# Second norm of a one-layer decoder step: x added on GpSimd ahead of the second projection part, squares taken at once, tile groups of 2, 2, 4, 4, 4, and 14 slots for the conditioning loads

## The chip, the cores and the metric

The kernel runs on one core of a Trainium2 chip. The metric is the device time of one execution in microseconds (us). TensorE (PE) multiplies matrices, VectorE (DVE) and ScalarE (ACT) work element by element, GpSimd (POOL) does some of that too, and SyncE (SP) issues most of the transfers (DMAs) from memory.

## The reference

One layer of a hybrid decoder over 256 prompt tokens and 8 samples of 4 tokens (288 columns in all), in float32. The conditioning vector gives six rows of shifts, scales and gates per sequence:

```
mod = silu(c) @ ada_w + ada_b
sh1, sc1, g1, sh2, sc2, g2 = split(mod, 6)
h = rms_norm(x) * (1 + sc1) + sh1
mix = token_mixer(h)            # ends with: out = merged @ w_out
x = x + g1 * mix
h = rms_norm(x) * (1 + sc2) + sh2
ff = conv_ffn(h)                # up = h @ w_up; conv, gelu, gate; @ w_down
x = x + g2 * ff
y = rms_norm(x, final_norm_w)
```

D_MODEL is 2048 (16 tiles of 128 rows), D_FF is 5632. The change concerns the stretch from the end of `merged @ w_out` to the first columns of `h @ w_up`: the residual sum, the second norm and its modulation, and the last eight blocks of `mod`.

## The kernel before

Activations lie transposed, 128 rows of a tile on the partitions and 288 token columns beside each other. A weight matrix is read in chunks of 512 rows by 256 columns (512 KB) into a ring `raw` of four. ScalarE rounds a chunk to its high part `whi` (line 1258, function `hi`), VectorE takes the low part `wlo` (line 1691, `lo`), and TensorE makes three products for each of eight (row tile, column half) pairs: high by high, high by low, low by high (lines 767 to 769). A chunk is 24 matmuls of 288 columns. The same split is made of the activations, `xh` and `xl`. The bank pair `ps` holds two output blocks in turn, and `bank_free` tells TensorE that a block has been read.

Each engine runs its own list of instructions in order, and semaphores join them. The order is written by hand.

The output projection has two passes. P1 (24 chunks) covers 12 of the 16 row tiles of `merged`; its results, times the gate g1, go to `mixo`. P2 (8 chunks, one for each output block u) covers the last four row tiles. `second_part(u)` on VectorE adds P2's result times the gate to `mixo` (line 2078, two operations out of PSUM), reads the sample columns into `x1s` (line 2079, which frees the bank) and adds them (line 2081). GpSimd then adds x, brought back from a spill into `xT2` (line 2399). ScalarE squares four tiles at a time (line 1611), and GpSimd sums the first twelve tiles' squares to four in `sqacc` (line 2404). TensorE sums the squares over the rows by multiplying with `ones` (line 1173): four times `sqacc` and four times the last tiles' squares. Square root on ScalarE (line 1286), reciprocal on VectorE (line 1841), then by groups of four tiles: normalise (line 1739, VectorE), sample columns modulated (lines 1750 and 1752, VectorE), prompt columns modulated (line 1304, ScalarE), high part (line 1310, ScalarE), low part (line 1758, VectorE). The first up chunk needs the first group, the second chunk the second, and so on.

Meanwhile the last eight blocks of conditioning are computed. A fill n is four chunks of `ada_w` (512 KB each) multiplied by the conditioning columns `cs` into a PSUM region (line 793); ScalarE copies the rows out (`fill_rows`, line 1261), TensorE turns them (`fill_turn`, line 746), VectorE reduces and stores them (`ada_block`, lines 1706 and 1713). Fills 0 and 1 lie inside P2, ahead of chunks 4 and 6; fills 2 and 3 behind P2, 4 and 5 behind the sum of squares, 6 and 7 ahead of up chunks 1 and 3. The turns of blocks 2 to 7 lie ahead of up chunks 3 to 8. The chunks of the fills land in ten slots taken in turn. SP issues them (line 693) between the up stream's loads (line 616), each behind the wait that its slot or ring place needs; a wait on SP holds up all that follows on it.

Between fill 5 and the first up chunk TensorE makes 16 transposes of the identity (`WARM`, line 1180). The up stream has 16 chunks for the first pair of blocks and ten more rounds of 16 in a loop; on ScalarE its step n makes the high part of chunk n + 3 first, then what else is due. GpSimd spills the new x from `xT2` to memory (line 2411) when the second group's low part is done; the down stream reads it again, and `ffl` later takes the place of `xT2`.

Of the kernel before, what the change touches and what calls it, by code (L numbers as in the profile page):

```python
# [21 lines left out]
P = 128  # L22
# [28 lines left out]
ZAB_Y = 4  # L51
# [69 lines left out]
FRING = 10  # L121
FILL_P2 = {4: 0, 6: 1}
FILL_UP = {1: 6, 3: 7}
# [53 lines left out]
WARM = 16  # L177
# [82 lines left out]
def build(nc, x_prompt, x_sample, c_prompt, c_sample, state_hgrn, state_mlstm_C, state_mlstm_n, state_mlstm_m,  # L260
# [5 lines left out]
    with ExitStack() as ctx:  # L266
# [143 lines left out]
        afill = sb("afill", [P, FRING - 4, KC, CN], stack=post)  # L410
# [148 lines left out]
        def fill_slot(e):  # L559


            r = e % FRING
            return araw[:, r] if r < 2 else top[:, r - 2] if r < 4 else afill[:, r - 4]

        def fill_landed(e):


            r = e // 2 % 5
            return (ld_x, 48) if r == 4 else (u_landed[r], 32 * UNITS + 16 * EXTRA * (r < 2))

        def fill_acc(n):


            o = CN * (n in (3, 4))
            return ab[:, 0:CN] if n in (0, 6) else R[:, (None, 2, 1, 1, 2, 2, None, 0)[n], o:o + CN]
# [38 lines left out]
        def _(sp):  # L614
# [74 lines left out]
            def fill_loads(a, b):  # L689
                for e in range(a, b):  # L690
                    if e >= FRING:
                        sp.wait_ge(a_used, before_a(A_UP) + e - FRING + 1 + FREE)
                    sp.dma_start(fill_slot(e), ada_v[:, KC * (e % 4):KC * (e % 4 + 1), bass.ds(CN * (A_UP + e // 4), CN)]).then_inc(fill_landed(e)[0], 16)
# [18 lines left out]
            first_up(0, 1, 2)  # L712
            fill_loads(10, 14)
            first_up(3)
            fill_loads(14, 24)
            first_up(4)
            fill_loads(24, 28)
            first_up(5)
            fill_loads(28, 32)
            first_up(*range(6, 16))  # L720
# [21 lines left out]
        def _(pe):  # L742
# [72 lines left out]
            def fill(n):  # L815
# [9 lines left out]
                if n == 6:  # L825
                    pe.wait_ge(ada_free, UNITS + A_UP - A_HG + 2 + FREE)
                if n == 7:
                    pe.wait_ge(rs_done, 3)
                for c in range(4):
                    e = 4 * n + c  # L830
                    if c % 2 == 0:
                        pe.wait_ge(fill_landed(e)[0], fill_landed(e)[1] + 32 * (e // FRING + 1))
# [6 lines left out]
            def stream(N, kinds, a0=None, steps=None, length=4, kt0=0, xparts=None, halves=None, start=False, ahead_of=None):  # L839

                steps = nothing() if steps is None else steps
                for k, kind in enumerate(kinds):
                    if kind == "s":
# [10 lines left out]
                        else:  # L854
                            if s == 0:
                                pe.wait_ge(bank_free[b % 2], N[1] + b // 2 + (PARTED // 2 - PARTED // 8) * start + FREE)
                            if xparts is not None and b == 0:
# [302 lines left out]
            def p2_ahead(q):  # L1160
                if q == 6:
                    fill_turn(0)
                if q in FILL_P2:
                    fill(FILL_P2[q])
            stream(N_P2, "s" * 8, length=1, kt0=12, halves=XS + 4, ahead_of=p2_ahead)
            fill(2)
            fill(3)
            fill_turn(1)
            pe.wait_ge(x1_acc, 3 + FREE)
            for t in range(8):  # L1170
                if t == 4:
                    pe.wait_ge(x1_sq, 4)
                x = mm(R[:, 0, 0:T], ones[:, :], sqacc[:, t, :] if t < 4 else mixo[:, 8 + t, :], start=t == 0, stop=t == 7)  # L1173
            x.then_inc(ms_done, 1)

            fill(4)
            pe.wait_ge(rs_done, 3)
            fill(5)
            for _ in range(WARM):
                nc.tensor.transpose(R[:, 0, 0:P], ident[:, :], ident[:, :])  # L1180

            def up_ahead(q):
                if q in FILL_UP:
                    fill(FILL_UP[q])
                if 3 <= q < 9:
                    fill_turn(q - 1)
            stream(up2_base(0), UP_KINDS, xparts=XS + 5, ahead_of=up_ahead)
# [59 lines left out]
        def _(act):  # L1247
# [44 lines left out]
            def modulate(nth, tmp, shift, scale, groups=range(4)):  # L1292

                if nth == 2:
                    act.wait_ge(sc_one, 1)
                for g in groups:
                    if nth == 1:
                        act.wait_ge(ada_free, 2 * g + 2 + FREE)
                    act.wait_ge(xn_done, 4 * (nth - 1) + g + 1)

                    parts = 2 if nth == 1 and g == 3 else 1
                    for t in range(4 * g, 4 * g + 4, 4 // parts):
# [3 lines left out]
                        act.wait_ge(md_p, XS * (nth - 1) + t // 4 + 1 + (t == 14))  # L1306
                        act.wait_ge(md_s, 2 * (4 * (nth - 1) + g + 1))
                        if g == 0 and nth == 2:
                            act.wait_ge(used, N_UP[0] + FREE)
                        A(xh[:, t:t + 4 // parts, :], tmp[:, t:t + 4 // parts, :], ACT.Copy).then_inc(xhi, 1)  # L1310

# [37 lines left out]
            modulate(1, merged, 0, KT, (0,))  # L1349
# [16 lines left out]
            for u in range(BESIDE, UNITS):  # L1366
                for h in range(4):
                    if h == 0 and u in (4, 6):
                        modulate(1, merged, 0, KT, (u // 2 - 1,))
# [6 lines left out]
            modulate(1, merged, 0, KT, (3,))  # L1376
# [220 lines left out]
            def fill_rows(n):  # L1597
                act.wait_ge(a_used, before_a(A_UP) + 4 * n + 4 + FREE)
                act.wait_ge(ada_cols, UNITS + A_UP - A_HG + n)
                if n == 6:  # L1600
                    act.wait_ge(ada_free, UNITS + A_UP - A_HG + n + FREE)
                ada_rows_of(fill_acc(n))

            def squares(n):
# [4 lines left out]
                if n % 2:  # L1609
                    act.wait_ge(x1_a, n + 1)  # L1610
# [3 lines left out]
            modulate(2, mixo, 3 * KT, 4 * KT)  # L1614

            def up_stream(N, kinds, first):
                def each(n):
                    i = first + n // 8
                    if isinstance(i, int) and 2 <= n < 8:
                        fill_rows(n)  # L1620
# [61 lines left out]
        def _(dve):  # L1682
# [150 lines left out]
            def modulate(nth, src, tmp, shift, scale):  # L1833
# [6 lines left out]
                dve.wait_ge(rs_done, 2 * nth - 1)  # L1840
                nc.vector.reciprocal(rstd[:, :], lnms[:, :]).then_inc(rs_done, 1)
                dve.wait_ge(rs_done, 2 * nth)
                for g in range(4):
                    normalise(nth, src, tmp, g)
                    samples(nth, tmp, g, shift, scale)
                    if g >= 2:
                        low_parts(nth, tmp, g - 2)
                low_parts(nth, tmp, 2)
                low_parts(nth, tmp, 3)
# [222 lines left out]
            def second_part(u):  # L2072
                b, kt = u % 2, slice(2 * u, 2 * u + 2)
                dve.wait_ge(used, N_P2[0] + u + 1 + FREE)
                dve.wait_ge(x1_m, u + 1)
                dve.wait_ge(bank_free[b], N_P1[1] + u // 2 + 1 + FREE)
                for m in range(2):
                    STT(mixo[:, 2 * u + m, 0:TP], ps[:, b, m, 0:TP], gate(u)[:, m, 0:1], mixo[:, 2 * u + m, 0:TP], ALU.mult, ALU.add).then_inc(x1_p, 1)  # L2078
# [401 lines left out]
```

## Time and profile before

| | us |
|---|---|
| median of 3 runs | 2236.93 (2236.75 to 2237.11) |
| profiled execution | 2236.46 |
| its span, first to last instruction | 2234.7 |
| TensorE busy | 2182.9 |
| VectorE busy | 1135.1 |
| ScalarE busy | 985.2 |
| GpSimd busy | 341.5 |

All times in the views are counted from the span's start. Busy time doesn't tell which engine sets the end: an engine that waits is not busy, and a busy engine may be covered by another. "Idle before" names what an engine waited for.

### The profile page before, as it was taken

The page shows a single profiled execution, that of the slowest core. Times are in us where ns is not written, and L with a number is a line of the kernel's source. Part 1 is how long each engine was busy: PE and PEld are TensorE (multiplying, and loading weights), DVE is VectorE, ACT ScalarE, POOL GpSimd, SP SyncE. Part 2 cuts the span into 40 slices and gives each one's busy share as a digit, 9 for nine tenths or more (in the row PEclk, how much of TensorE's full clock was granted, in tenths as well). Part 3 has the DMA queues.
Part 4 walks back from the last instruction along what each step waited for, and adds up shares of the span by engine and source line. Part 5 has one row for each costly group of instructions (what it writes and reads, how often), then busy time and mean ns, then how long its engine had stood idle before and what let it go on. Part 6 is the DMA issues. An engine that isn't in the chain of part 4 may idle for free. (4 is left out here: it accounts for less than half of the span.)

```text
span 2234.7 us, 42265 instructions
## 1 busy us (share of the span) xinstructions
PE 2182.9 (98%) x17250; PEld 2057.4 (92%) x17250; DVE 1135.1 (51%) x1597; ACT 985.2 (44%) x1365; POOL 341.5 (15%) x524
## 2 busy tenths in 40 slices
PE   6899999999999999999999998999999999999997
PEld 3589999999999999999999987999999999999997
DVE  3356465564565444444445566555555555444443
ACT  3336563564454344454535335434434444433332
POOL 2000311322222221121212241000000000010000
PEclk9999999999999999999999999999999999999999
DMA  9987666667676767668676698555555555555553
GB/s 350 376 282 217 200 198 205 205 197 217 200 223 196 230 184 229 214 207 250 210 216 204 210 302 276 159 172 160 163 167 160 169 166 160 179 162 175 172 168 106
DMA packets 407411, 460.03 MB, mean 206 GB/s; under 512 B 14843, under 2 KB 379955, under 8 KB 406433
## 3 DMA queue, kind: packets, MB, share of 16 engines
q1 hardware_dynamic: 394192, 410.64, 58.4%
q0 software_dynamic: 12240, 46.03, 6.7%
q8 instruction: 109, 1.79, 0.3%
q10 hardware_dynamic: 833, 1.26, 0.2%
q14 instruction: 37, 0.30, 0.0%
HBM read 431.48 MB, written 26.39 MB: 205 GB/s over the span
## 5 line engine op out<-in xcount | busy, mean ns | idle before, releaser
L767 PE MATMUL ps<-xh,whi 128*128 128x288 f32 x3968 | 1191.5, 300 | 13.5 <-issue 6.6
L1691 DVE TENSOR_TENSOR wlo<-raw,whi 128x1024 fp32r<-128x1024 f32 x584 | 735.9, 1261 | 908.0 <-ACT whi L1258 905.9
L769 PE MATMUL ps<-xh,wlo 128*128 128x288 f32 x3968 | 1173.2, 296 | 0.0
L768 PE MATMUL ps<-xl,whi 128*128 128x288 f32 x3968 | 1173.1, 296 | 0.0
L1258 ACT ACTIVATE whi<-raw 128x1024 fp32r<-128x1024 f32 x584 | 616.5, 1057 | 761.9 <-PE ps L769 717.8
L767 PEld LDWEIGHTS ps<-xh,whi 128*128 128x128 f32 x3968 | 747.3, 188 | 55.4 <-issue 39.9
L768 PEld LDWEIGHTS ps<-xl,whi 128*128 128x128 f32 x3968 | 747.8, 188 | 0.0
L769 PEld LDWEIGHTS ps<-xh,wlo 128*128 128x128 f32 x3968 | 747.2, 188 | 0.0
L767 PE MATMUL ps<-ffh,whi 128*128 128x288 f32 x704 | 208.5, 296 | 0.0
L769 PE MATMUL ps<-ffh,wlo 128*128 128x288 f32 x704 | 208.0, 295 | 0.0
L768 PE MATMUL ps<-ffl,whi 128*128 128x288 f32 x704 | 207.9, 295 | 0.0
L767 PEld LDWEIGHTS ps<-ffh,whi 128*128 128x128 f32 x704 | 132.5, 188 | 0.3
L769 PEld LDWEIGHTS ps<-ffh,wlo 128*128 128x128 f32 x704 | 132.3, 188 | 0.0
L768 PEld LDWEIGHTS ps<-ffl,whi 128*128 128x128 f32 x704 | 132.1, 188 | 0.0
L2430 POOL COPY tails<-abuf 128x4 f32 x22 | 4.2, 189 | 419.0 <-ACT abuf L1626 419.0
L2320 POOL TENSOR_TENSOR S<-S,AC 128x1024 f32<-128x1024 f32 x16 | 32.3, 2020 | 148.6 <-PE R L1030 148.6
L1632 ACT ACTIVATE ffh<-yb 128x576 f32 (+1 forms) x22 | 15.1, 686 | 69.7 <-DVE yb L2113 69.7
L2106 DVE SCALAR_TENSOR_TENSOR acv<-abuf,par,acv 128x304 f32<-128x304 f32 x88 | 41.1, 528 | 0.0
L1261 ACT ACTIVATE arows<-ab 128x256 f32<-128x256 f32 x26 | 10.0, 384 | 62.4 <-PE ab L793 60.6
L793 PE MATMUL ab<-araw,cs 128*32 128x256 f32 x544 | 36.4, 385 | 0.0
L2425 POOL COPY abuf<-cst 128x16 f32 x44 | 21.1, 511 | 98.6 <-DVE acv L2106 91.0
L1625 ACT ACTIVATE abuf<-ps 128x512 f32<-128x512 f32 x22 | 13.2, 599 | 50.0 <-PE ps L769 50.0
(422 smaller groups left out, 1629.9 us busy)
## 6 DMA issues: line engine op xcount, KB each, us to landing
raw<-in_w_in SPq DMA_DIRECT2D x288, 512.0 KB, 4.7
raw<-in_w_up SPq DMA_DIRECT2D x176, 512.0 KB, 3.5
raw<-in_w_down SPq DMA_DIRECT2D x88, 512.0 KB, 3.4
araw<-in_ada_w SPq DMA_DIRECT2D x74, 512.0 KB, 5.8
uraw_x<-in_ada_w SPq DMA_DIRECT2D x36, 512.0 KB, 10.0
raw<-in_w_out SPq DMA_DIRECT2D x32, 512.0 KB, 3.5
top<-in_ada_w SPq DMA_DIRECT2D x24, 512.0 KB, 8.2
afill<-in_ada_w SPq DMA_DIRECT2D x18, 512.0 KB, 7.1
```

What stands on the lines that cost most here:

```text
L767: mm(o, whi[:, s, kk, cols], hi[:, kt0 + kk, :], start=first and kk == 0, stop=False)
L768: mm(o, whi[:, s, kk, cols], lo[:, kt0 + kk, :], start=False, stop=False)
L769: x = mm(o, wlo[:, s, kk, cols], hi[:, kt0 + kk, :], start=False, stop=last and kk == KC - 1)
L793: x = mm(acc[32 * kk:32 * kk + 32, 0:CN], cs[:, kt0 + kk, :], weights[:, kk, :], start=first, stop=last)
L1258: A(whi[:, s], raw[:, s], ACT.Copy).then_inc(hi_done, 1)
L1261: A(arows0[:, :], acc[:, 0:CN], ACT.Copy).then_inc(ada_rows, 1)
L1625: A(abuf[:, :, 2:2 + TP], ps[:, 0, :, 0:TP], ACT.Copy)
L1632: A(ffh[:, bass.ds(2 * i, 2), :], yb[:, :, :], ACT.Copy).then_inc(ff_hi, 1)
L1691: TT(wlo[:, s], raw[:, s], whi[:, s].bitcast(F32), ALU.subtract).then_inc(lo_done, 1)
L2106: STT(acv[:, m, 0:AB - 2], abuf[:, m, w:w + AB - 2], cw[w][:, c1], acv[:, m, 0:AB - 2], ALU.mult, ALU.add).then_inc(ff_conv, 1)
L2320: G(S0[:, :, :], S0[:, :, :], rep_last(AC[:, 3, j, :], P), ALU.mult).then_inc(hg["scaled"], 1)
L2425: x = nc.gpsimd.tensor_copy(seq(abuf[:, m, 2 + TP:AB], 2 + LS)[:, :, 0:2], cst[:, bass.ds(2 * i + m, 1), :].rearrange("p o (b j) -> p (o b ...
```

## The change

GpSimd adds x to `mixo` before the second part, all eight pairs of tiles in a row, and `second_part` writes the finished x into `xT2`; ScalarE squares from there, the last two pairs singly, and GpSimd sums twelve tiles' squares with two operations instead of a memset and three. Fills 2, 3 and 4 and the turn of block 1 stand behind the sum of squares, the transposes of the identity are gone, and fills 5, 6 and 7 stand ahead of up chunks 1, 6 and 9. The modulation goes by groups of 2, 2, 4, 4 and 4 tiles, and the first up chunk waits for its two halves. Three low parts of up weights move behind the second parts on VectorE. The slots become 14, four of them in `merged`, and SP's order of loads follows. The spill of x waits for the third group instead of the second.

```
-FRING = 10
+FILL_SLOTS = tuple(range(14)) + tuple(range(10)) + (0, 1, 4, 5, 6, 7, 12, 13)
 FILL_P2 = {4: 0, 6: 1}
-FILL_UP = {1: 6, 3: 7}
+FILL_UP = {1: 5, 6: 6, 9: 7}
+TURN_UP = {3: 2, 4: 3, 5: 4, 6: 5, 7: 6, 10: 7}
+ROWS_UP = {2: 2, 3: 3, 4: 4, 5: 5, 6: 6, 9: 7}
+NORM2_GROUPS = ((0, 2), (2, 4), (4, 8), (8, 12), (12, 16))
...
 # SP
             fill_loads(4, 10)
-            first_up(0, 1, 2)
+            first_up(0, 1)
+            sp.wait_ge(xlo, XS + 5)
             fill_loads(10, 14)
+            first_up(2)
+            fill_loads(14, 18)
             first_up(3)
-            fill_loads(14, 24)
-            first_up(4)
-            fill_loads(24, 28)
-            first_up(5)
-            fill_loads(28, 32)
-            first_up(*range(6, 16))
+            fill_loads(18, 22)
+            first_up(4, 5)
+            fill_loads(22, 28)
+            first_up(6)
+            fill_loads(28, 30)
+            first_up(7)
+            fill_loads(30, 32)
+            first_up(*range(8, 16))
...
 # TensorE
             def p2_ahead(q):
+                if q in FILL_P2:
+                    fill(FILL_P2[q])
                 if q == 6:
                     fill_turn(0)
-                if q in FILL_P2:
-                    fill(FILL_P2[q])
             stream(N_P2, "s" * 8, length=1, kt0=12, halves=XS + 4, ahead_of=p2_ahead)
-            fill(2)
-            fill(3)
-            fill_turn(1)
-            pe.wait_ge(x1_acc, 3 + FREE)
+            pe.wait_ge(x1_acc, 2 + FREE)
             for t in range(8):
-                if t == 4:
-                    pe.wait_ge(x1_sq, 4)
+                if t in (4, 6):
+                    pe.wait_ge(x1_sq, 2 + t // 2)
                 x = mm(R[:, 0, 0:T], ones[:, :], sqacc[:, t, :] if t < 4 else mixo[:, 8 + t, :], start=t == 0, stop=t == 7)
             x.then_inc(ms_done, 1)
+            fill(2)
+            fill_turn(1)
+            fill(3)
             fill(4)
-            pe.wait_ge(rs_done, 3)
-            fill(5)
-            for _ in range(WARM):
-                nc.tensor.transpose(R[:, 0, 0:P], ident[:, :], ident[:, :])
...
-                if 3 <= q < 9:
-                    fill_turn(q - 1)
-            stream(up2_base(0), UP_KINDS, xparts=XS + 5, ahead_of=up_ahead)
+                if q in TURN_UP:
+                    fill_turn(TURN_UP[q])
+            stream(up2_base(0), UP_KINDS, xparts=XS + 6, halves=XS + 6, ahead_of=up_ahead)
...
 # ScalarE: squares(n) at step n of P2
-                if n % 2:
-                    act.wait_ge(x1_a, n + 1)
+                    for u in (6, 7):
+                        act.wait_ge(x1_p, 3 * (u + 1))
+                        A(mixo[:, 2 * u:2 * u + 2, :], xT2[:, 2 * u:2 * u + 2, :], ACT.Square).then_inc(x1_sq, 1)
+                elif n % 2:
+                    act.wait_ge(x1_p, 3 * (n + 1))
                     A(mixo[:, 2 * n - 2:2 * n + 2, :], xT2[:, 2 * n - 2:2 * n + 2, :], ACT.Square).then_inc(x1_sq, 1)
...
 # VectorE: modulate, the new order
+                lo(N_P2, 5 + LEAD)
+                lo(N_P2, 6 + LEAD)
+                dve.wait_ge(rs_done, 3)
                 nc.vector.reciprocal(rstd[:, :], lnms[:, :]).then_inc(rs_done, 1)
+                dve.wait_ge(rs_done, 4)
+                normal(0)
+                sampled(0)
+                normal(1)
+                sampled(1)
+                low(0)
+                normal(2)
+                low(1)
+                sampled(2)
+                normal(3)
+                sampled(3)
+                low(2)
+                ada_block(A_UP + 1, ab, ada_free, CN)
+                normal(4)
+                sampled(4)
+                low(3)
+                lo(N_P2, 7 + LEAD)
+                low(4)
...
 # VectorE: second_part and its loop
-                dve.wait_ge(x1_m, u + 1)
-                dve.wait_ge(bank_free[b], N_P1[1] + u // 2 + 1 + FREE)
+                dve.wait_ge(x1_a, u + 1)
                 for m in range(2):
-                    STT(mixo[:, 2 * u + m, 0:TP], ps[:, b, m, 0:TP], gate(u)[:, m, 0:1], mixo[:, 2 * u + m, 0:TP], ALU.mult, ALU.add).then_inc(x1_p, 1)
+                    STT(xT2[:, 2 * u + m, 0:TP], ps[:, b, m, 0:TP], gate(u)[:, m, 0:1], mixo[:, 2 * u + m, 0:TP], ALU.mult, ALU.add).then_inc(x1_p, 1)
...
-            stream(N_P2, "s" * 8, each=second_part)
-            modulate(2, xT2, mixo, 3 * KT, 4 * KT)
+            for u in range(8):
+                if u < 5:
+                    lo(N_P2, u + LEAD)
+                second_part(u)
+                if u == 6:
+                    ada_block(A_UP, ab, ada_free, CN)
+            modulate(xT2, mixo, 3 * KT, 4 * KT)
...
 # GpSimd
-            nc.gpsimd.memset(sqacc[:, :, :], 0.0).then_inc(zab, 1)
             pool.wait_ge(back_x, 16)
             for u in range(8):
                 kt = slice(2 * u, 2 * u + 2)
-                pool.wait_ge(x1_p, 3 * (u + 1))
-                G(xT2[:, kt, :], xT2[:, kt, :], mixo[:, kt, :], ALU.add).then_inc(x1_a, 1)
-                if u % 2 and u < 7:
...
+                pool.wait_ge(x1_m, u + 1)
+                pool.wait_ge(bank_free[u % 2], N_P1[1] + u // 2 + 1 + FREE)
+                G(mixo[:, kt, :], mixo[:, kt, :], xT2[:, kt, :], ALU.add).then_inc(x1_a, 1)
+            pool.wait_ge(x1_sq, 2)
+            G(sqacc[:, :, :], mixo[:, 0:4, :], mixo[:, 4:8, :], ALU.add).then_inc(x1_acc, 1)
+            pool.wait_ge(x1_sq, 3)
+            pool.wait_ge(x1_acc, 1 + FREE)
+            G(sqacc[:, :, :], sqacc[:, :, :], mixo[:, 8:12, :], ALU.add).then_inc(x1_acc, 1)
...
-            pool.wait_ge(xlo, XS + 7)
+            pool.wait_ge(x1_p, 24)
+            pool.wait_ge(xlo, XS + 8)
             pool.dma_start(x1_spill, xT2[:].rearrange("p a b -> p (a b)")).then_inc(back_x, 16)
```

## Rows read from the trace of the kernel before

**Rows 1.** Page: busy us of TensorE; costliest groups (busy, mean ns | idle before).
```profile
PE 2182.9 (98%) x17250; PEld 2057.4 (92%) x17250; DVE 1135.1 (51%) x1597; ACT 985.2 (44%) x1365; POOL 341.5 (15%) x524
...
L1691 DVE TENSOR_TENSOR wlo<-raw,whi 128x1024 fp32r<-128x1024 f32 x584 | 735.9, 1261 | 908.0 <-ACT whi L1258 905.9
...
L1258 ACT ACTIVATE whi<-raw 128x1024 fp32r<-128x1024 f32 x584 | 616.5, 1057 | 761.9 <-PE ps L769 717.8
```

**Rows 2.** Windows: engines' busy us, granted clock (PEclk), DMA share, GB/s, by stretch.
```profile
1347.80:1351.40 3.60, 3.58 (x12) 2.15 (x16) 0.00 (x0) 0.00 (x0) 0.00 (x0) 0.60 1.10 350
1361.26:1364.50 3.24, 3.24 (x17) 3.24 (x18) 3.02 (x4) 3.21 (x6) 0.00 (x0) 0.64 1.09 349
```

**Rows 3.** TensorE in order of time: start, us, line, records [idle before, releaser].
```profile
1305.09 0.38 PE L767 MATMUL ps<-xh,whi 128*128 128x288 f32 x1
...
1318.00 1.07 PE L793 MATMUL ab<-araw,cs 128*32 128x256 f32 x16
1318.89 1.05 PE L793 MATMUL ab<-top,cs 128*32 128x256 f32 x16
1320.56 0.40 PE L767 MATMUL ps<-xh,whi 128*128 128x288 f32 x1 [0.63 <-DVE x1s L2079]
...
1328.28 0.41 PE L746 MATMUL ab<-ident,arows 128*128 128x128 f32 x2 [1.08 <-ACT arows L1261]
...
1342.84 0.44 PE L746 MATMUL ab<-ident,arows 128*128 128x128 f32 x2 [1.81 <-DVE mod L1713]
1343.12 2.11 PE L1173 MATMUL R<-sqacc,ones 128*128 128x288 f32 x8
1347.82 3.59 PE L1173 MATMUL R<-mixo,ones 128*128 128x288 f32 x8 [2.60 <-ACT mixo L1611]
...
1355.18 1.97 PE L1180 MATMUL R<-ident 128*128 128x128 f32 x16
1361.26 0.37 PE L767 MATMUL ps<-xh,whi 128*128 128x288 f32 x1 [4.11 <-issue]
...
1394.25 0.38 PE L746 MATMUL ab<-ident,arows 128*128 128x128 f32 x2
```

**Rows 4.** VectorE in order of time, P2 and the second norm.
```profile
1316.68 2.91 DVE L1691 TENSOR_TENSOR wlo<-raw,whi 128x1024 fp32r<-128x1024 f32 x1 [3.68 <-ACT whi L1258]
1319.52 0.86 DVE L2078 SCALAR_TENSOR_TENSOR mixo<-ps,mod,mixo 128x256 f32<-128x256 f32 x2
...
1354.04 1.36 DVE L1739 TENSOR_TENSOR mixo<-xT,rstd 128x1152 f32<-128x1152 f32 x1
...
1359.81 1.35 DVE L1758 TENSOR_TENSOR xl<-mixo,xh 128x1152 fp32r<-128x1152 f32 x1
```

**Rows 5.** GpSimd in P2; the add's durations are min/median/max in ns.
```profile
L2399 POOL TENSOR_TENSOR xT<-xT,mixo x8: 1396/1426/2345, 1310.0 to 1345.2; 128x576 f32<-128x576 f32 x8
...
1306.33 0.57 POOL L2368 DMA_DIRECT2D out<-Cp  x1
...
1315.84 2.68 POOL L2404 TENSOR_TENSOR sqacc<-sqacc,mixo 128x1152 f32<-128x1152 f32 x1 [1.33 <-issue]
```

**Rows 6.** ScalarE in order of time, first group of the modulation.
```profile
1355.49 2.08 ACT L1304 ACTIVATE mixo<-mixo,mod 128x256 f32<-128x256 f32 x4 [3.54 <-DVE mixo L1739]
1357.60 1.16 ACT L1310 ACTIVATE xh<-mixo 128x1152 fp32r<-128x1152 f32 x1
```

**Rows 7.** VectorE and GpSimd in an earlier stage; VectorE's operation over all (min/median/max ns).
```profile
332.81 4.20 DVE L1909 SCALAR_TENSOR_TENSOR SQ<-SQ,lbc,X 128x384 f32<-128x384 f32 x4
...
335.14 0.93 POOL L2289 TENSOR_TENSOR KH<-WQ,AC 128x256 f32<-128x256 f32 x1
...
L1909 DVE SCALAR_TENSOR_TENSOR SQ<-SQ,lbc,X x16: 605/610/2255, 211.0 to 647.3; 128x384 f32<-128x384 f32 x16
```

**Rows 8.** Transfers: SP's first fill loads behind P1; issues of the spill, us to landing.
```profile
1311.71 4.55 SPq L693 DMA_DIRECT2D afill<-in_ada_w  x6
...
x_spill<-xT POOLq DMA_DIRECT2D x1, 2304.0 KB, 9.2
```

## What I expect of the change

> **What bounds the kernel now.** I read the page's busy table first: TensorE is busy for 98% of the span [rows 1], so only what keeps TensorE from its own work can shorten the run. I then listed TensorE in order of time from the second part of the output projection (P2, from 1305.1) to the last conditioning turn in the first up block (1394.25 to 1394.6) [rows 3]. Everything the diff touches lies there, and behind it the up and down streams run without gaps.
>
> That stretch is 89.5 us long. Its work: P2's first four chunks take 12.9 us, from 1305.1 to 1318.0, so 3.25 each, and 16 chunks (eight of P2, eight of the up stream) take 52. A conditioning fill is two groups of 16 records (1.07 each, overlapping a little), 1.9 us, and a turn 0.35 [rows 3]: eight of each are 15.2 and 2.8. The sum over the squares is 16 records; the eight at full clock took 2.1, so 4.2. Together 74.2, so some 15 us are not work. The gaps say where [rows 3]: 0.6 before P2's fifth chunk, 1.1 before the first turn and about 0.3 behind it, 1.8 before the second turn, 2.6 before the last squares; then 1.5 because the granted clock had fallen (0.60, towards the lower level of 1.2 GHz [rows 2]) and eight records took 3.6 instead of 2.1; 1.9 of warming transposes; 4.1 of idling before the first up chunk, and about 1.7 more in that chunk, whose start ran at clock 0.64 [rows 2]. With 0.4 at a later turn that is 16.0, and all that the change can win.
>
> The idling hangs on one chain. TensorE finishes the sum at 1351.4; square root and reciprocal end at 1354.0, the first four tiles are normalised by 1355.4 [rows 4], modulated on ScalarE (2.1) and rounded (1.16) by 1358.8 [rows 6], and VectorE takes their low part only at 1359.8, after two further groups, done at 1361.2 [rows 4]. That is 9.85 us, and only two fills lie over it.
>
> One resource beside TensorE is full: the DMA queues move 350 GB/s there [rows 2].
>
> **The change, part by part.** *x added on GpSimd early.* The eight adds go ahead of the second parts, and the squares no longer wait for GpSimd. One add takes 1.43 [rows 5], eight 11.4. They can't start before GpSimd has issued its last state store, at 1306.9 [rows 5]; the removed memset stood right behind. Here is the cost: GpSimd and VectorE hold each other off. A low part (wlo, 1.26 in the mean [rows 1]) took 2.91 while the sum of squares ran on GpSimd [rows 4, 5]. What happens to many waiting on both sides is to be seen in an earlier stage: there the first of four VectorE operations, 0.61 each when free, was held for up to 2.26 by one GpSimd operation, but all four were through after 4.20, at 337.0, while GpSimd was still inside a string of operations and itself held (0.93 for 256 elements, more than half of an add of 576) [rows 5, 7]. I read that as taking turns. So I let each VectorE operation with two SBUF inputs wait for at most one add; the multiply-adds out of PSUM (0.86 a pair) ran beside GpSimd at their usual pace [rows 4].
>
> By turns: adds and low parts alternate from 1307.9 to 1322.1. VectorE's x1s frees the bank for P2's chunk 4 at 1320.3, for chunk 5 at 1324.5 (its square, 1.17, and high part, 1.06, stand in order on ScalarE [rows 1, 6]) and for chunk 6, behind the first sum on GpSimd (2.7), at 1331.0. TensorE loses 0.4, 0.9 and 0.9; before it lost 2.0 in the same place. P2 therefore ends at 1337.5, as before. Bounds: with no holding off, 2.3 earlier; if GpSimd's eight adds shut VectorE out until 1319.2, the bank for chunk 3 is late by 6.9, some of it absorbed by the fills, and P2 ends 3.5 later.
>
> A rule speaks against this part: the Trainium skill, GPSIMD Engine Reference, section 4.1 (Engine selection), gives elementwise adds to VectorE and calls GpSimd about twice as slow with two inputs. The trace agrees on the price: 1.43 for 576 elements, against half of VectorE's 1.36 for 1152 [rows 4, 5]. By that rule the adds would put some 5.4 us on VectorE during P2 and none on GpSimd, an estimate from those rows; what decides is whether TensorE waits, and by turns it waits about as long as before.
>
> *Squares at once, sums.* Two fills leave the place ahead of the norm. Pair 7's multiply-adds, x1s and tail follow P2's end by 1.4, its square of 576 by 0.7 more. TensorE meanwhile does six of the eight sums (3.2), so nothing waits: the sum ends at 1337.5 + 4.2 = 1341.7, against 1351.4.
>
> *Groups of 2, 2, 4, 4, 4; fills 2, 3, 4 and a turn behind the norm.* From the sum's end: 2.65 to the reciprocal's end, where the first normalise starts [rows 3, 4], 0.75 for two tiles, 1.1 and 0.7 on ScalarE (half of [rows 6]), 0.75 for the low part, handovers: 6.1. Over it lie three fills and a turn, 6.05. So chunk 0 of the up stream starts at 1347.8 at full clock, against 1361.3; the warming transposes go. If the fills' data came late, each us would show.
>
> *What is late next.* VectorE and ScalarE need about 3.3 per group of four tiles, a chunk's time, but VectorE now also carries three low parts of weights and a conditioning block. In their order: low(1) is done at 1349.75, so chunk 0 waits 0.4 at its half. low(2) ends at 1353.8; fill 5 lies over that, chunk 1 starts at 1353.9. low(3) ends at 1357.45 and the weights' low part for chunk 2, queued behind it, at 1358.65: a wait of 1.6. Chunk 2 ends at 1362.0; turn 2 waits for ScalarE's rows until 1362.4, chunk 3 ends at 1366.0.
>
> *14 slots, order of loads.* A load of 0.52 MB takes 1.5 us at 350 GB/s. From the first of the queue (issued 1311.7 [rows 8], 1.1 allowed for what is in flight) the nth lands at 1312.8 + 1.5n. The slots bring no byte sooner, as the DMA was full already; they let SP issue loads 10 to 13 and their successors past fills that moved behind the norm. The last chunk of fill 4 is 20th: 1342.8, needed at 1346.8. The last of fill 5 is 26th: 1351.8, needed at 1352.4. Up chunk 6 is 31st, 7 is 34th, 8 is 37th. But the spill of x1 (2304 KB, 9.2 to landing [rows 8]) now starts with low(2), at 1353.8, beside a full queue, and takes 2.36 MB / 350 GB/s = 6.7, nearly all of it ahead of chunk 6: that lands at about 1365.7, chunk 7 at 1370.2. ScalarE's high part of chunk 6 stands ahead of the rows of turn 3, on which TensorE waits: 1365.7 + 1.06 for the high part + 0.5 for the rows (one of the four in [rows 6]) is 1367.2, a wait of 1.2. In the same way turn 4 waits for chunk 7 until 1371.75, 1.0. Bounds: loads undisturbed, neither waits (2.2 less); the spill's whole 9.2 ahead of them, 2.8 more.
>
> *Fills 6 and 7 at the 7th and 10th chunk.* Turn 4 and chunk 5 end at 1375.35, fill 6 at 1377.25, turn 5 waits 0.3 for VectorE, chunk 6 ends at 1381.1, turn 6 and chunk 7 at 1384.7. Fill 7 and turn 7 are still to do, 2.25: 1386.95 against 1394.6. Saved: 7.7 us. All later work moves up with it.
>
> **The rivals.** *B: gentler.* VectorE and GpSimd collide little and the spill doesn't stand before the loads: 7.7 + 2.3 + 2.2 = 12.2, 2224.7. For it: the multiply-adds out of PSUM go on beside GpSimd; against it: the 2.91 of [rows 4] and the full DMA.
>
> *C: the new burst costs more.* Either GpSimd shuts VectorE out (3.5) or the spill goes wholly first (2.8): about 4.5 saved, 2232.5. For it: adds stand ready with nothing between them. Against it: the turns of [rows 7].
>
> *D: slower.* The spill decides: every us that up chunk 6 lands behind 1365.7 comes one to one onto TensorE through ScalarE's order. Slower by over 0.2% (4.5 us here, about what a measurement can tell from no change) needs 7.7 + 4.5 = 12.2, so a landing at 1378. From 1353.8 that would be 2.36 MB and 3.7 loads at 178 GB/s; the rows show 350. The time would be 2241.5.
>
> *E: no gain.* The loads are the true bound, and TensorE only waits elsewhere. The 38 loads up to chunk 9 and the spill end at 1312.8 + 57 + 6.7 = 1376.5, and chunk 9 isn't wanted before 1386: only with 10 us more would this be so, 2236.9.
>
> **How the numbers follow.** The profiled execution took 2236.46 about its span of 2234.7, the median of three 2236.93. The saving is made on the profiled one and taken off the median: 2236.93 - 7.7 = 2229.2. My chances: forecast 0.50 (own range 2227 to 2231.5), B 0.23, C 0.19, E 0.05, D 0.03. The range reaches over B and C, 2223.5 to 2234.5. Faster by over 0.2% means under 2232.5: the forecast, B and half of C, 0.80 with some of the forecast's own spread given off; same, the rest of C and E, 0.16; slower 0.04.
>
> **What would show it.** In the profile after: P2 ending near 1337.5 with VectorE's low parts stretched to 2 to 2.7 beside GpSimd's adds; the sum's 16 records without a gap, ending near 1341.7; the first up chunk at 1347.8 with the clock at 1.00; waits of a us or two at chunk 2 and at turns 3 and 4, with ScalarE idle for the load of chunk 6. I am wrong if low parts of VectorE stay blocked over several adds, if a TensorE gap of 2 us or more brings the clock down again, or if the loads land at another pace than 1.5 us each.

## The result, and the profile after

| | before | after |
|---|---|---|
| median, us | 2236.93 (13 runs, 2235.23 to 2238.81) | 2240.65 (13 runs, 2239.75 to 2242.47) |
| ratio after to before | | 1.0018 [1.0011, 1.0025] |
| span of the profiled execution, us | 2234.7 | 2238.9 |

The change costs 0.18%: too little to call by the 0.2% set above, but its interval lies wholly above 1. The forecast was 2229.2, the range 2223.5 to 2234.5. The range missed, by 6 us.

The page first [rows 1]: TensorE's busy time is 2 us up, and ahead of the first of its three products (L792) it now idles 8.2 us for one releaser, VectorE's x1s; [rows 3] of before show 0.63 for the same releaser.

```profile
PE 2184.9 (98%) x17234; PEld 2059.9 (92%) x17234; DVE 1141.7 (51%) x1601; ACT 985.5 (44%) x1367; POOL 335.3 (15%) x522
...
L792 PE MATMUL ps<-xh,whi 128*128 128x288 f32 x3968 | 1194.0, 301 | 16.7 <-DVE x1s L2135 8.2
```

GpSimd in order of time [rows 5]: the eight adds stand back to back, 1.37 each, with no wait among them (a string, below).

```profile
1306.70 0.57 POOL L2427 DMA_DIRECT2D out<-Cp  x1
1307.28 10.97 POOL L2458 TENSOR_TENSOR mixo<-mixo,xT 128x576 f32<-128x576 f32 x8
```

VectorE in order of time [rows 4]: one low part (1.22 when free) lasts from before the first add until 1.1 behind the last one's end at 1318.25, and all of second_part waits behind it. Below, the stretch of turn 3: ScalarE and VectorE hang on one load there.

```profile
1306.99 12.35 DVE L1719 TENSOR_TENSOR wlo<-raw,whi 128x1024 fp32r<-128x1024 f32 x1 [0.42 <-ACT whi L1277]
1319.26 0.86 DVE L2134 SCALAR_TENSOR_TENSOR xT<-ps,mod,mixo 128x256 f32<-128x256 f32 x2
1320.05 0.21 DVE L2135 TENSOR_TENSOR x1s<-ps,mod 128x64 f32<-128x64 f32 x1
1320.29 0.23 DVE L2137 TENSOR_TENSOR xT<-mixo,x1s 128x64 f32<-128x64 f32 x1
1320.43 1.22 DVE L1719 TENSOR_TENSOR wlo<-raw,whi 128x1024 fp32r<-128x1024 f32 x1
...
1376.62 1.22 DVE L1719 TENSOR_TENSOR wlo<-raw,whi 128x1024 fp32r<-128x1024 f32 x1 [4.27 <-ACT whi L1277]
1377.76 0.23 DVE L1734 TENSOR_REDUCE msum<-ab 128x18 f32<-128x72 f32 x1
1378.02 0.18 DVE L1741 TENSOR_TENSOR mod<-msum,par 128x18 f32<-128x18 f32 x1
```

ScalarE at the same place, its wait for the load of up chunk 6:

```profile
1375.53 1.06 ACT L1277 ACTIVATE whi<-raw 128x1024 fp32r<-128x1024 f32 x1 [5.16 <-DMA raw<-in_w_up]
1376.49 0.36 ACT L1280 ACTIVATE arows<-R 128x256 f32<-128x256 f32 x1
```

TensorE in order of time [rows 3]: P2's chunk 2 waits 8.25; the sum is gapless; up chunk 0 starts at 1356.49; half of fill 5 waits for data; turn 3 waits 4.15.

```profile
1320.31 0.61 PE L792 MATMUL ps<-xh,whi 128*128 128x288 f32 x1 [8.25 <-DVE x1s L2135]
...
1346.30 2.10 PE L1193 MATMUL R<-sqacc,ones 128*128 128x288 f32 x8
1348.23 2.10 PE L1193 MATMUL R<-mixo,ones 128*128 128x288 f32 x8
...
1356.49 0.37 PE L792 MATMUL ps<-xh,whi 128*128 128x288 f32 x1 [0.33 <-DVE xl L1878]
...
1362.69 1.07 PE L818 MATMUL R<-afill,cs 128*32 128x256 f32 x16 [1.49 <-DMA afill<-in_ada_w]
...
1378.26 0.69 PE L771 MATMUL ab<-ident,arows 128*128 128x128 f32 x2 [4.15 <-DVE mod L1741]
```

The windows [rows 2] add two things. From 1311.8, while VectorE is still blocked, no byte moves (0 GB/s), and behind these two long waits of TensorE the granted clock is at the lower level, 1.2 GHz: 0.50 until 1325.8, 0.51 in the up chunk behind turn 3. Each slow stretch costs about 2.4 us: 23 records 0.24 apart instead of 0.133 in the first, a chunk of 5.8 us instead of 3.4 in the second.

```profile
1311.80:1320.30 8.50, 0.26 (x2) 0.03 (x1) 8.47 (x5) 0.00 (x0) 6.45 (x5) 0.72 0.00 0
1320.30:1325.80 5.50, 5.49 (x23) 5.49 (x24) 3.29 (x7) 2.11 (x2) 0.00 (x0) 0.50 0.96 323
...
1376.00:1380.00 4.00, 1.74 (x8) 1.75 (x9) 1.55 (x3) 1.59 (x5) 0.47 (x3) 0.63 1.09 366
1380.00:1384.00 4.00, 4.00 (x19) 4.00 (x19) 3.00 (x7) 1.20 (x2) 0.00 (x0) 0.51 1.09 379
```

Why no byte moves, the transfer queue says [rows 8]: the last load of w_out waits for the ring place that the blocked low part holds, and the fills stand behind it on SP. They start at 1319.78 instead of 1311.71.

```profile
1319.37 0.37 SPq L636 DMA_DIRECT2D raw<-in_w_out  x1
1319.78 6.31 SPq L713 DMA_DIRECT2D afill<-in_ada_w  x6
```

### The profile page after: what moved, and what is told of

It is laid out like the page before. It is cut to its first block, busy times and chain, and to the rows that moved or that the text cites. A ratio compares the mean times of both kernels' runs of the same rounds, so it can differ in the third digit from the quotient of the medians.

```text
span 2238.9 us, 42241 instructions
## 1 busy us (share of the span) xinstructions
PE 2184.9 (98%) x17234; PEld 2059.9 (92%) x17234; DVE 1141.7 (51%) x1601; ACT 985.5 (44%) x1367; POOL 335.3 (15%) x522
## 4 chain that ended last, share of the span: by engine, by line
PE 94%; DMA 2%; DVE 1%; issue 1%; ACT 1%; SPq 0%; DVEq 0%; ACTq 0%
PE ps L792 28%; PE ps L794 27%; PE ps L793 27%; PE R L771 3%; PE ab L818 2%; DMA uraw_x<-in_ada_w 1%; PE R L923 1%; PE R L1061 1%; DMA raw<-in_w_in 0%; PE R L1010 0%; PE R L1034 0%; PE ab L771 0%; PE ps L923 0%; PE R L1046 0%; DMA raw<-in_w_up 0%
## 5 line engine op out<-in xcount | busy, mean ns | idle before, releaser
L792 PE MATMUL ps<-xh,whi 128*128 128x288 f32 x3968 | 1194.0, 301 | 16.7 <-DVE x1s L2135 8.2
L1719 DVE TENSOR_TENSOR wlo<-raw,whi 128x1024 fp32r<-128x1024 f32 x584 | 744.3, 1275 | 906.2 <-ACT whi L1277 904.1
L792 PEld LDWEIGHTS ps<-xh,whi 128*128 128x128 f32 x3968 | 748.9, 189 | 59.3 <-issue 36.9
L792 PE MATMUL ps<-ffh,whi 128*128 128x288 f32 x704 | 208.5, 296 | 0.0
L792 PEld LDWEIGHTS ps<-ffh,whi 128*128 128x128 f32 x704 | 132.5, 188 | 0.3
```

What stands on the lines that cost most here:

```text
L792: mm(o, whi[:, s, kk, cols], hi[:, kt0 + kk, :], start=first and kk == 0, stop=False)
L1719: TT(wlo[:, s], raw[:, s], whi[:, s].bitcast(F32), ALU.subtract).then_inc(lo_done, 1)
```

## The experiments

Every ratio is against runs of the kernel before on the same chip; its medians on the four chips used were 2237.03, 2236.86, 2237.48 and 2237.19 us. Edits are to the changed kernel unless another is named.

**Is it the string of adds?** Four kernels take it away in four ways. e1_paced lets an add start only when a low part has ended (the last three wait for the same one):

```
+                if u:
+                    pool.wait_ge(lo_done, N_P2[0] + min(u + 2, 7) + 1)
```

> Each of GpSimd's adds from the second on waits for the low part of weights that VectorE takes just before, so VectorE gets in between. Theory S (GpSimd kept VectorE out for all eight adds; the empty DMA queue, the late loads and the low clock follow from that): the longest low part in P2 falls from 12.35 to under 3 us, the DMA gap from 1311.8 to 1320.3 goes, and the time is 2227 to 2231. Rival R (the stretch is too full of transfers in any case, and being shut out only moved the wait): the gap goes, but turn 3 waits longer for the load of up chunk 6, and the time is 2234 to 2238.

Measured: 2232.58 us, ratio 0.998 [0.9971, 0.9989]. In e2_dve_add the same eight adds run on VectorE:

```
+            def add_x(u):                    # called ahead of second_part(u)
...
+                TT(mixo[:, kt, :], mixo[:, kt, :], xT2[:, kt, :], ALU.add).then_inc(x1_a, 1)
...
-                G(mixo[:, kt, :], mixo[:, kt, :], xT2[:, kt, :], ALU.add).then_inc(x1_a, 1)
```

> The eight adds of x are made by VectorE, each just ahead of its second part; GpSimd does none of them. Theory S: nothing blocks VectorE, which carries 8 x 0.75 = 6 us more in P2 (about 3.3 per chunk, a chunk's time), so P2 loses at most 2 us and the time is 2228 to 2232. Rival R: 2234 to 2238, as in the paced one.

Measured: 2233.08, 0.998 [0.9971, 0.9989]; an add takes 0.75 there. e3_chain keeps everything on GpSimd, and each add only waits until the one before it has ended:

```
+                if u:
+                    pool.wait_ge(x1_a, u)
```

> Each add on GpSimd waits only for the add ahead of it to have finished, nothing else is changed. If GpSimd keeps VectorE out because its adds are handed on without a pause, the wait is a pause in which the low part gets in: low parts of 2 to 3 us and 2228 to 2232. If GpSimd wins whenever both stand ready, or the pause is too short, the low part of 12 us stays and the time is 2239 to 2242.

Measured: 2232.9, 0.998 [0.9971, 0.9989]. e4_late_add undoes the early add alone (the squares and their sums move to match, not shown):

```
-                    STT(xT2[:, 2 * u + m, 0:TP], ps[:, b, m, 0:TP], gate(u)[:, m, 0:1], mixo[:, 2 * u + m, 0:TP], ALU.mult, ALU.add).then_inc(x1_p, 1)
+                    STT(mixo[:, 2 * u + m, 0:TP], ps[:, b, m, 0:TP], gate(u)[:, m, 0:1], mixo[:, 2 * u + m, 0:TP], ALU.mult, ALU.add).then_inc(x1_p, 1)
...
-                G(mixo[:, kt, :], mixo[:, kt, :], xT2[:, kt, :], ALU.add).then_inc(x1_a, 1)
+                pool.wait_ge(x1_p, 3 * (u + 1))
+                G(xT2[:, kt, :], xT2[:, kt, :], mixo[:, kt, :], ALU.add).then_inc(x1_a, 1)
```

> The early add alone is undone: second parts go to mixo as before, GpSimd adds them to x behind, the squares wait for that; all else is as changed. Theory S: no burst, P2 ends near 1338, the last pair's add (1.43) lies ahead of its square, so the sum waits about 1 to 2 us; the time is 2228 to 2233. Rival R: 2234 to 2238.

Measured: 2232.17, 0.9978 [0.9969, 0.9987]. All four lie at 2232 to 2233: the string costs about 8 us, and adding x early gains nothing here, since e4 without it is no slower than e3 with it. Three of the four came out somewhat slower than expected; that rest is taken up below. In e3's trace a pause of 0.17 us is enough, first on GpSimd (two of seven like it):

```profile
1307.18 1.44 POOL L2460 TENSOR_TENSOR mixo<-mixo,xT 128x576 f32<-128x576 f32 x1
1308.79 2.22 POOL L2460 TENSOR_TENSOR mixo<-mixo,xT 128x576 f32<-128x576 f32 x1 [0.17 <-POOL mixo L2460]
1311.17 2.34 POOL L2460 TENSOR_TENSOR mixo<-mixo,xT 128x576 f32<-128x576 f32 x1 [0.17 <-POOL mixo L2460]
```

then on VectorE: the first low part waits for one add (1.44 + 1.2 of its own), and the second and third add are held in turn.

```profile
1306.87 2.84 DVE L1719 TENSOR_TENSOR wlo<-raw,whi 128x1024 fp32r<-128x1024 f32 x1 [0.41 <-ACT whi L1277]
...
1311.01 1.21 DVE L1719 TENSOR_TENSOR wlo<-raw,whi 128x1024 fp32r<-128x1024 f32 x1
```

**How many pauses, and is it the likeness of the adds?** e8_chain_at4 has one, ahead of the fifth add:

```
+                if u == 4:
+                    pool.wait_ge(x1_a, u)
```

> The changed kernel with one wait: the fifth of GpSimd's adds waits for the fourth to have finished; the other adds follow each other without a wait. If a string of adds without a wait keeps VectorE out until its end, the first low part takes four adds and itself, about 6.9 us (12.35 with eight, 2.84 with one), a second one is held as long, and the time lies between, 2234 to 2238. If one pause anywhere is enough to make them take turns, or the string's length doesn't matter, low parts of under 3 us and 2232 to 2233.

Measured: 2236.05, 0.9996 [0.9987, 1.0005]. The time is that of the first theory, but only half of what it says came: the first four adds hold a low part for 6.96 us; the second low part, beside the last four, wasn't held as long and takes 2.44 although nothing pauses among them:

```profile
1308.28 6.96 DVE L1719 TENSOR_TENSOR wlo<-raw,whi 128x1024 fp32r<-128x1024 f32 x1 [0.41 <-ACT whi L1277]
...
1316.50 2.44 DVE L1719 TENSOR_TENSOR wlo<-raw,whi 128x1024 fp32r<-128x1024 f32 x1
```

So in e9_chain_at1 the one pause stands behind the first add (`if u == 1`).

> The changed kernel with one wait in the string of adds: the second waits until the first has ended. One-pause theory (in the run with the wait on the fifth add alone, VectorE got in between the sixth and the seventh add too, where there is no wait: once an add of GpSimd has itself been held, the string lets VectorE in after each add): low parts of 2 to 3 us throughout and 2231 to 2234 us. Pause-each-time theory (VectorE gets in only where GpSimd waits): the second low part is held over six adds, about 8 us, and the time is 2235 to 2238 us.

Measured: 2233.29, 0.998 [0.9971, 0.9989]. The seven adds behind the pause have no other; the low parts beside them take 2.47, 1.60 and 2.46, and the adds take turns with them. GpSimd's rows, then two of VectorE's:

```profile
1308.63 1.44 POOL L2460 TENSOR_TENSOR mixo<-mixo,xT 128x576 f32<-128x576 f32 x1
1310.24 12.50 POOL L2460 TENSOR_TENSOR mixo<-mixo,xT 128x576 f32<-128x576 f32 x7 [0.17 <-POOL mixo L2460]
...
1312.46 2.47 DVE L1719 TENSOR_TENSOR wlo<-raw,whi 128x1024 fp32r<-128x1024 f32 x1
...
1318.48 1.60 DVE L1719 TENSOR_TENSOR wlo<-raw,whi 128x1024 fp32r<-128x1024 f32 x1 [2.18 <-ACT whi L1277]
```

This is what the one-pause theory expects. It isn't shown that the pause is what changes the string; the last section has another reading. e10_shapes has no pause, but unlike neighbours, after the earlier stage [rows 7]:

```
-                G(mixo[:, kt, :], mixo[:, kt, :], xT2[:, kt, :], ALU.add).then_inc(x1_a, 1)
+                for h in range(2 * u, 2 * u + 1 + u % 2):
+                    w = slice(h, h + 2 - u % 2)
+                    x = G(mixo[:, w, :], mixo[:, w, :], xT2[:, w, :], ALU.add)
+                x.then_inc(x1_a, 1)
```

> The changed kernel, with no wait, but every second add cut into two of one tile each, so that neighbours differ in shape: twelve operations in place of eight. Shape theory (an earlier stage with unlike operations let VectorE through, so unlike neighbours let it in): low parts of 2 to 3 us and 2231 to 2234 us. Pause theory (only a wait of GpSimd, or an add of it that is itself held, lets VectorE in): the first low part is held until the last of the twelve has ended, 12.5 to 14 us, and the time is 2239 to 2244 us.

Measured: 2240.64, 1.0016 [1.0007, 1.0025], as the changed kernel. The low part is held over eleven of the twelve adds; it ends at 1319.09, and the last add, 1.76 instead of 0.8, is held by it.

```profile
1306.94 12.15 DVE L1719 TENSOR_TENSOR wlo<-raw,whi 128x1024 fp32r<-128x1024 f32 x1 [0.43 <-ACT whi L1277]
```

The shape theory is out. That VectorE got in ahead of the twelfth fits neither theory.

**Where is the rest?** e3 is still 3.7 us above the forecast. In its trace fill 5 waits 3.5 us for its last load, and turn 3 waits 1.9. e5_rows (on e3) takes the rows on ScalarE and the block on VectorE ahead of the next chunk's high and low part in the first up block, so that turn 3 doesn't hang on the load of up chunk 6 (ScalarE's half is shown, VectorE's is alike):

```
 # ScalarE's and VectorE's stream(..., ahead_of=None), ahead of hi and of lo
+                    if ahead_of is not None:
+                        ahead_of(n)
...
-                    if isinstance(i, int) and n in ROWS_UP:
-                        fill_rows(ROWS_UP[n])
+            def rows_ahead(n):
+                if n in ROWS_UP:
+                    fill_rows(ROWS_UP[n])
```

> On top of the chained adds (2232.9): in the first up block ScalarE copies a conditioning block's rows ahead of its high part, and VectorE stores the block ahead of its low part, so neither stands behind the load of up chunk 6. Theory Q (turn 3 waits for that load only through the order on ScalarE and VectorE): turn 3 no longer waits (1.9 us now), the clock stays up in chunk 4 (1.6), and the time is 2228 to 2231. Rival R (transfers bound the stretch): the same wait comes back in front of up chunk 6, and the time is 2232 to 2234.

Measured: 2229.0, 0.9965 [0.9953, 0.9977], as theory Q has it, and turn 3 no longer waits. e6_loads (on e3) loads fill 5's last two chunks ahead of up chunks 4 and 5:

```
-            fill_loads(18, 22)
+            fill_loads(18, 24)
             first_up(4, 5)
-            fill_loads(22, 28)
+            fill_loads(24, 28)
```

> On top of the chained adds: the last two loads of fill 5 are issued ahead of up chunks 4 and 5 instead of behind them, nothing else. Theory Q: fill 5's second half waits 3.5 us for them now and at most 1 us then; with the clock that dips behind it the time is 2228 to 2231. Rival R: what is won there is waited for again at turn 3, and the time is 2232 to 2234.

Measured: 2232.49, 0.9981 [0.9972, 0.999]. The wait only moved: TensorE's idle time for the data of fills 4 and 5 falls from 4.1 us to 1.8, that ahead of turn 3 rises from 1.9 to 6.8.

```profile
1371.33 0.47 PE L771 MATMUL ab<-ident,arows 128*128 128x128 f32 x1 [6.82 <-DVE mod L1741]
```

e7_both joins the two.

> Chained adds, rows and blocks first, and the two loads first. Theory Q: both waits are gone, 2225 to 2228. Rival R: the waits move to up chunk 6 or fill 6, 2229 to 2232.

Measured: 2228.7, 0.9965 [0.9951, 0.9979], between the two expectations and no better than e5. What it still waits for is up chunk 6's load, behind the spill of x: turn 4 waits 3.05 us, since its rows on ScalarE and the block ahead of it on VectorE stand behind that chunk's high and low part (the next expectation calls it turn 3).

```profile
1370.40 0.69 PE L771 MATMUL ab<-ident,arows 128*128 128x128 f32 x2 [3.05 <-DVE mod L1744]
```

e11_spill (on e7) issues the spill later, on GpSimd behind its memset:

```
-            pool.dma_start(x1_spill, xT2[:].rearrange("p a b -> p (a b)")).then_inc(back_x, 16)
...
             nc.gpsimd.memset(abuf[:, :, 0:2], 0.0).then_inc(zab, 1)
+            pool.wait_ge(lo_done, N_UP[0] + 6)
+            pool.dma_start(x1_spill, xT2[:].rearrange("p a b -> p (a b)")).then_inc(back_x, 16)
```

> The kernel with both orders changed (e7_both), and the spill of x issued once the low part of up chunk 5 is done instead of the third group's. Load theory (the spill's bytes stand before fill 5's last loads and up chunk 6's, and turn 3 waited 3.1 us for that and lost about 1.2 to the lower clock behind it): those waits go, 2223.5 to 2226 us. Rival (the spill overlapped loads that wait for ring places and slots anyway): 2228 to 2229.5 us.

Measured: 2229.44, 0.9967 [0.9955, 0.9979]: the rival's time. Turn 4 no longer waits, but turn 6 now waits 4.27: ScalarE, which copies its rows, stands before up chunk 8's load, issued just behind the spill.

```profile
1375.90 1.06 ACT L1277 ACTIVATE whi<-raw 128x1024 fp32r<-128x1024 f32 x1 [8.29 <-DMA raw<-in_w_up]
...
1379.39 0.30 PE L771 MATMUL ab<-ident,arows 128*128 128x128 f32 x1 [4.27 <-ACT arows L1280]
```

e12_spill_at7 (on e11) waits two chunks longer (`N_UP[0] + 8`).

> The kernel with both orders changed and the spill two up chunks later than in e11_spill: issued once the low part of up chunk 7 is done. In e11_spill the wait of turn 3 went, but ScalarE then waited 8.3 us for up chunk 8's load, which was issued just behind the spill; the time stayed. Load theory (the spill's 2.36 MB stand before whichever up chunk is loaded behind them, and by up chunk 9 there is room in the queue): no turn waits more than 1 us and the time is 2224 to 2227 us. Rival (the stretch is full of bytes up to there, so the wait moves on to up chunk 9 or 10): 2228 to 2230 us.

Measured: 2223.81, 0.9941 [0.9928, 0.9955], faster than both kernels and a little below the load theory's range. The windows of its trace, 15 us each: the DMA queues stay full until 1380, with the spill issued at 1369.85 instead of e7's 1352.85, the clock stays at 1.00, and TensorE idles only 1.07 us behind 1365, at turn 5.

```profile
1350.00:1365.00 15.00, 14.20 (x123) 12.60 (x122) 12.80 (x18) 12.75 (x20) 0.10 (x1) 1.00 1.08 346
1365.00:1380.00 15.00, 13.93 (x124) 12.77 (x124) 9.07 (x19) 6.85 (x9) 2.83 (x8) 1.00 1.06 393
1380.00:1395.00 15.00, 15.00 (x132) 13.91 (x131) 6.85 (x10) 5.08 (x6) 0.00 (x0) 1.00 0.59 192
```

## Why the prediction was wrong

Starts on TensorE in us; the columns of runs are shifted so that GpSimd's last state store is issued at 1306.33 as in before (by 0.37, 0.26 and 1.47). The forecast's chunk 9 is its 1386.95, behind fill 7 and turn 7, with two chunks of 3.25.

| | forecast | after | e3_chain | e12_spill_at7 |
|---|---|---|---|---|
| sum ends | 1341.7 | 1350.0 | 1339.0 | 1339.0 |
| up chunk 0 | 1347.8 | 1356.1 | 1345.5 | 1346.1 |
| up chunk 1 | 1353.9 | 1363.3 | 1355.3 | 1352.2 |
| turn 3 | 1367.2 | 1377.9 | 1369.0 | 1362.5 |
| turn 4 | 1371.75 | 1383.9 | 1374.0 | 1365.9 |
| up chunk 9 ends (before: 1401.0) | 1393.5 | 1404.7 | 1394.8 | 1387.8 |

*The step that failed* is "I read that as taking turns. So I let each VectorE operation with two SBUF inputs wait for at most one add". One low part waited for all eight. e1 to e4 show that this, and not the rest of the change, costs the 8 us; in e9, with one pause, turns are taken, as forecast. The working also let the first low part through ahead of the adds, which then alternate with the next ones from 1307.9. A row of before spoke against that: a low part that began 0.34 us ahead of a GpSimd operation, while GpSimd was issuing a transfer, waited for the whole of it (4.12 us instead of 1.22).

```profile
399.45 0.95 POOL L2302 DMA_DIRECT2D S<-in_state_hgrn  x1
400.42 2.68 POOL L2285 TENSOR_TENSOR WG<-SG 128x1152 f32<-128x1152 f32 x1
...
400.08 4.12 DVE L1691 TENSOR_TENSOR wlo<-raw,whi 128x1024 fp32r<-128x1024 f32 x1 [4.22 <-ACT whi L1258]
```

All three of the prediction's signs of being wrong came: a low part blocked over several adds, long gaps of TensorE with a lower clock behind them, and loads at another pace.

*The bound on that step was too small as well.* The prediction had the shut-out, until 1319.2 (it was 1319.3 for the low part's end), and gave it 3.5 us "some of it absorbed by the fills". The sum ended 8.3 late: about 8.25 of waiting and 2.4 of lower clock behind it, less the 2.2 of smaller waits that the forecast had in P2 and that didn't come. Since the first low part was the blocked one, the chunk that waited was chunk 2 and not chunk 3, by 8.25 instead of 6.9, and nothing absorbed it: the fills stand behind it in TensorE's own order. Had rival C carried about 8 us, its time would have been near 2237, and the range would have reached higher; the loads make the other 3.5. What the bound didn't ask either is who waits for a blocked low part besides TensorE: SP did, and the transfers stood still for 8.5 us in which those of before moved 317 GB/s.

*The loads were the second mis-sized term*: "the nth lands at 1312.8 + 1.5n". In e3, with no stop, fill 5's last load came 1.7 us behind the forecast's 1351.8 (the fill's second half ran at 1353.5, shifted as in the table), and turn 3 was 1.8 late. In the changed kernel fill 5 cost 1.1 and turn 3 another 1.3 against the forecast, and the slow chunk behind it 1.4. The spill's term was right in kind (the spill stands before up chunk 6) and too small: 2.2 us of waits, where e12, which moves the spill alone from e7's place, is 4.9 us below e7. The prediction also hung turn 3 on ScalarE's order alone; VectorE's block, behind the low part of chunk 6, holds it too [1377.76 above]; e5 moved both, and neither was moved alone.

*Right:* the place of the gain and the chain behind the norm. The sum is gapless; chunk 0 starts 6.15 behind it (forecast 6.1), over the three fills and the turn, at full clock; chunk 2 didn't wait the 1.6 forecast. With the string broken, e3's P2 and sum beat the forecast by 2.7, as rival B had it (2.3), and lost that again on the loads.

*The rivals.* C's first mechanism is what happened. D's time, 2241.5, is within 1 us of the measured one, but by chance: up chunk 6 did come 9.5 late, near 1375.2, and turn 3 waited 4.15 for it, yet most of that is the stop of the transfers and not the spill; e4 and e3 have the same spill and are faster than before. E, the loads as the true bound, was given 0.05 and is part of what stood between e3 and e12: e6 and e11 show a wait moving from one load to the next with no gain. The other part was the order on ScalarE and VectorE, which e5 changed.

*The rule on engines.* The prediction weighed the Trainium skill, GPSIMD Engine Reference, section 4.1 (Engine selection), which gives such adds to VectorE. e2 did so: 0.75 us an add against GpSimd's 1.44, and 2233.08 against e3's 2232.9. The rule's price agrees, and it decides nothing here; what decided was the string.

## What to carry to other kernels

Ask of every string of GpSimd operations what two-input VectorE work falls beside it, and break the string behind its first operation with a wait on its own semaphore: 0.17 us here bought 7, and a break ahead of the fifth of eight bought 4.6. When an engine can be blocked, price the block through everything in order behind it, the loads and the clock included, and not only through the matmul that waits. Where a stretch is full of transfers, moving one load ahead can just move the wait to the next (e6); move out what isn't wanted there, as the spill, and far enough (e12, not e11).

## What was not expected of the hardware

GpSimd's string kept VectorE out as a whole: 12.35 us for a low part over eight adds, 6.96 over four, 12.15 over eleven of unlike shapes. In e9, after one pause of 0.17 in which VectorE got in and the next add was itself held (2.2 instead of 1.4), the adds let VectorE in without any further pause.

By the records the low part that was shut out had begun 0.3 us ahead of the first add and yet was the one to wait. In the kernel before, one that began 0.23 ahead of an add, with GpSimd idle until then, was not held, and the add was (2.28); the one at 400.08, above, was. In both places shown here where VectorE began first and lost, GpSimd was issuing a transfer just then [1306.70 and 399.45 above].

```profile
1309.74 1.22 DVE L1691 TENSOR_TENSOR wlo<-raw,whi 128x1024 fp32r<-128x1024 f32 x1
...
1309.97 2.28 POOL L2399 TENSOR_TENSOR xT<-xT,mixo 128x576 f32<-128x576 f32 x1 [2.00 <-DVE mixo L2081]
```

That leaves a reading without a lasting effect of the pause, which no run tests: the pause lets in the low part that waits there, and the later ones get in because they begin in the middle of the string. In the runs above, every low part that was shut out of a string had begun ahead of it. Every VectorE operation that got in between two operations of GpSimd with no wait between them had begun in the middle of the string; e10's is the one exception. In e1 one got in like that although the string of three has no pause inside and none of its adds was held, and so did the held operation of the earlier stage [rows 7], which began 0.25 us behind GpSimd's first. A run in which a low part begins in the middle of the unbroken string of eight would tell the two readings apart.

```profile
1325.33 4.20 POOL L2460 TENSOR_TENSOR mixo<-mixo,xT 128x576 f32<-128x576 f32 x3 [3.67 <-DVE wlo L1719]
1326.11 0.73 DVE L2137 TENSOR_TENSOR xT<-mixo,x1s 128x64 f32<-128x64 f32 x1
...
333.09 2.08 POOL L2320 TENSOR_TENSOR S<-S,AC 128x1024 f32<-128x1024 f32 x1 [5.56 <-PE R L1030]
333.34 2.25 DVE L1909 SCALAR_TENSOR_TENSOR SQ<-SQ,lbc,X 128x384 f32<-128x384 f32 x1
```

e10's twelfth add has a hint of its own. The waits ahead of the adds, on GpSimd's queue, were passed by 1306.9 in the changed kernel, ahead of the low part's 1306.99; in e10 the last was passed at 1307.0, behind the low part's 1306.94, and VectorE got in between the two adds that follow this last wait. But in e1 the waits of all three adds had been passed as well when VectorE got in, so this alone isn't the cause either.

```profile
L2457 POOLq EVENT_SEMAPHORE  x8: 17/17/43, 1306.2 to 1306.9; - x8
...
L2457 POOLq EVENT_SEMAPHORE  x8: 17/17/43, 1306.2 to 1307.0; - x8
```

The Trainium skill, SBUF — State Buffer, section "SBUF: two separate sides", says that whichever starts first has the pair of ports for one whole instruction. The runs agree for single adds (e3's low part of 2.84 is 0.31 ahead of the add, the add's 1.44 and 1.09 behind it, near its own 1.22), and differ on the string and, by the records, on who starts first beside a transfer's issue. What makes the difference stays open.
